# Opening of a two-layer encoder: lighter VectorE work, matrices loaded as rows, power factors on GpSimd

## The chip, the core and the metric

The kernel runs on one core of one Trainium2 chip. The time is the device time of one execution in microseconds (us). The engines are TensorE (PE), VectorE (DVE), ScalarE (ACT), GpSimd (POOL) and the DMA queues, which SyncE (SP), ScalarE and GpSimd feed. All run side by side and wait for each other through semaphores.

## What is computed

A trunk of two pre-norm layers over 256 tokens of width 1024, in float32. Cut to what the change touches:

```python
proj = rms_norm(x, norm_mix[layer]) @ w_in[layer]     # q, k, v, u, gates
q, k = rotary(q), rotary(k)                           # x1*cos - x2*sin, x2*cos + x1*sin per half head
lam = exp(sum(lp[0] * lp[1])) - exp(sum(lp[2] * lp[3])) + lam_init
for direction in range(2):                            # bidirectional diagonal state space mixer
    a_bar = exp(lam_ssm * dt)                         # complex, 32 groups x 64 states
    b_bar = ((a_bar - 1) / lam_ssm)[..., None] * b_mat
    states = linear_scan(a_bar, b_bar @ u)            # 256 steps, reversed in direction 1
    y = y + real(c_mat @ states)
y = y + u * d_skip
```

After each mixer stands a feed-forward part: a SwiGLU in layer 0, top 2 of 8 experts in layer 1.

## The kernel before

Each weight tile (128 x 2048 numbers, 1 MB) is loaded by SyncE, rounded by ScalarE (`hi`, L1215) and its rest taken by VectorE (`lo`, L1632, a split); TensorE then multiplies three times (hi hi, hi lo, lo hi, L657). The order on each engine is written out by hand and the same in both layers: a function `mixer(l)` per engine. A tile's `hi` waits until TensorE has used the tile two before it, and a projection in PSUM (banks PJ) starts when VectorE or ScalarE has signalled `pj_free` for the one before.

The state space mixer works on chunks of four tokens. It needs the input matrices times a_bar to the powers 0 to 4 (`input_power` on VectorE in layer 0, `product` on GpSimd in layer 1), the output matrices likewise (`c_chain`, GpSimd) and tables of phases (`phasors`, `phase_products`, GpSimd; ScalarE mirrors them in `scan_tables`, L1326 and L1332). `inner` (L767, L776, TensorE) forms the products within a chunk; it waits for VectorE's diagonal (`kdiag_ready`), for VectorE's last input power (`b_part`) and for GpSimd's last output power (`c_ready`, the memset of L2232). Then TensorE transposes the input powers (the B turns: eight banks, each evacuated by ScalarE, L1253; ScalarE's mirror copies for the first step stand between the fourth and the fifth). After them comes the loop over eight half heads with scores, softmax, scan steps and the projections of the gates.

In layer 0 the opening runs so. Parameters of the states are worked out as rows and transposed by TensorE into one bank (`par`, L675, seven transposes, before projection t + 2); VectorE copies it (L2002). GpSimd waits for this copy, then does phasors 1 and 2, `c_chain`, phasors 3 and 4, the first phase products. VectorE, after a product and a sum for the attention's lambda (L1998, L1999), works out the four factors co * a^k (`next_factor`, L1734 to L1737, 4 operations each), waits for the raw input matrices, and does power 0; power 1 waits until ScalarE has read the last two banks of the output matrices ("ct", L1308), since it writes where they were loaded. Then come splits, powers 2 to 4, the diagonal and the rotary of q and k in turn. The input matrices are loaded by GpSimd in eight transfers whose runs are 16 numbers, and copied by ScalarE to PSUM banks PY (L1373); the output matrices are loaded twice, in four transfers, so that a 128 x 128 transpose gives both halves. `rotary` multiplies q by cos into SBUF (L1692), the crossed halves by sin into SBUF (L1695, then `pj_free`) and adds the two (L1700).

Of the kernel before, what the change touches and what calls it, by code (L numbers as in the profile page):

```python
# [18 lines left out]
P = 128  # L19
# [23 lines left out]
C_ID, C_TRI, C_ONE, C_IOTA, C_SEL, C_COS, C_SIN = 0, 128, 256, 384, 513, 641, 769  # L43
C_ROW, C_SLOT, C_END = 897, 899, 900
# [79 lines left out]
def build(nc, x, norm_mix, w_in, attn_lambda, attn_subln, ssm_lam_re, ssm_lam_im, ssm_log_dt, ssm_b_re, ssm_b_im,  # L124
# [6 lines left out]
    with ctx:  # L131
# [66 lines left out]
        braw, bbar = powers(area(0, 1024)), powers(area(TMP + 2048, 1024))  # L198
        bt = [powers(area(1024 + 1024 * i, 1024)) for i in range(2)]
        pt = [powers(area(c0, 1024)) for c0 in (14592, TMP)]  # L200
        craw = [area(c0, 1024).rearrange("p (i a s) -> p i a s", i=8, a=2) for c0 in (8192, TMP + 1024)]
# [206 lines left out]
        dve_mark, power_mark = small[:, 20:21], small[:, 21:22]  # L408
        dve_rows, sel_early, inv_ready = sem("dve_rows"), sem("sel_early"), sem("inv_ready")
        B_LOADS, C_LOADS = 16 * 8, 16 * 4  # L410
        den_ready, radius_ready, c_in = sem("den_ready"), sem("radius_ready"), sem("c_in")
# [243 lines left out]
        def _(pe):  # L655
# [137 lines left out]
            def states_numbers_t(l):  # L793

                pe.wait_ge(c_in, C_LOADS * (l + 1))
                for g in range(4):
                    transposes((l, "ct", g), [craw[g // 2][:, 4 * (g % 2) + i, :, :].rearrange("p a s -> p (a s)") for i in range(4)])
# [34 lines left out]
            def mixer(l):  # L832
# [7 lines left out]
                if l == 0:  # L840
                    pe.wait_ge(dve_par, 1)
                    pe.wait_ge(radius_ready, 1)
                    transposes("par", [row(PACK + i) for i in range(7)])
# [364 lines left out]
        def _(act):  # L1208
# [92 lines left out]
            def state_numbers(l):  # L1301

                for g in range(4):
                    bank = wait_turn(act, (l, "ct", g))
                    r, d = g // 2, g % 2
                    for odd in range(2):
                        rows = slice(64 * odd, 64 * (odd + 1))
                        m = act.activation(cblk[rows, r, :, 7 * d, :],  # L1308
                                           bank[rows, :].rearrange("p (j g h) -> p j g h", g=2, h=GC)[:, :, odd, :],
                                           ACT.Copy, scale=1.0 if r == 0 else -1.0)  # L1310
# [30 lines left out]
            def mixer(l):  # L1341
# [28 lines left out]
                if l == 0:  # L1370
                    act.wait_ge(b_in, B_LOADS)
                    for r in range(2):
                        act.activation(PY[r][:, :], braw[:, r].rearrange("p q d h -> p (q d h)"), ACT.Copy).then_inc(braw_full, 1)  # L1373
                    state_numbers(0)
# [251 lines left out]
        def _(dve):  # L1626
# [55 lines left out]
            def rotary(l, name, dst):  # L1682
                i = place_of(l, name)

                cos_t, sin_t = (cst[:, c:c + 128].rearrange("p (t c) -> p t c", t=2) for c in (C_COS, C_SIN))
                for th in range(TH):
                    if th == 0:
                        dve.wait_ge(pj0_full, use(l, i) + 1)
                    else:
                        dve.wait_ge(tile_used, T_MIX[l] + 2 * i + 2)  # L1690
                    src = PJ[th][:, :]
                    own.step(stt(a_flat[:, 0:512].rearrange("p (h c) -> p h c", c=HD), src.rearrange("p (h c) -> p h c", c=HD),  # L1692
                                 col(RI + th), cos_t[:, th, :].unsqueeze(1).broadcast_to([P, 8, HD]), MUL, MUL))
                    for a in range(2):
                        m = stt(a_flat[:, 512:1024].rearrange("p (h a c) -> p h a c", a=2, c=32)[:, :, a, :],  # L1695
                                src.rearrange("p (h a c) -> p h a c", a=2, c=32)[:, :, 1 - a, :], col(RI + th),
                                sin_t[:, th, 32 * a:32 * (a + 1)].unsqueeze(1).broadcast_to([P, 8, 32]), MUL, MUL)
                    m.then_inc(pj_free[th], 1)
                    dve.wait_ge(pj_free[th], pj_read(l, i))
                    tt(dst[:, th, :], a_flat[:, 0:512], a_flat[:, 512:1024], ADD).then_inc(rot_ready, 1)  # L1700
                    dve.wait_ge(rot_ready, 4 * l + (0 if name == "q" else 2) + th + 1)

# [26 lines left out]
            def next_factor(k):  # L1729

                def times(i):
                    return par[:, i:i + 1, 0:32].broadcast_to([P, 2, 32])
                src = par[:, CO_RE:CO_IM + 1, 0:32] if k == 0 else coef[:, k - 1]
                tt(coef_tmp[0], src, times(A_RE), MUL)  # L1734
                own.step(tt(coef_tmp[1], src[:, ::-1, :], times(A_IM), MUL))
# [678 lines left out]
```

## Time and profile before

| | us |
|---|---|
| median of 3 runs (1413.34 to 1413.91) | 1413.44 |
| the profiled execution | 1413.13 |
| its span in the trace | 1411.3 |
| TensorE busy | 1371.2 (97%) |
| VectorE busy | 1107.8 (78%) |
| ScalarE busy | 895.1 (63%) |
| GpSimd busy | 358.3 (25%) |

The shares are means over the whole span, and the stretch that the change touches is its first tenth: between 40 and 80 us VectorE and GpSimd are each busy for more than 19 of every 20 us. What is to be read is which engine ends last there. The chain of waits answers that: it goes back from the last instruction, at each step to what released it. The timeline lists the instructions of an engine in order; a bracket gives the idle time before an instruction and what ended it. An fp32 matmul stands as two records in it, a transpose as one.

### The profile page before, as it was taken

What the parts mean: (1) busy time and instruction counts of PE and PEld (TensorE: products, weight loads), DVE (VectorE), ACT (ScalarE), POOL (GpSimd) and SP (SyncE); (2) the same over time, 40 slices, a digit from 0 to 9 for tenths busy, and PEclk for the clock granted to TensorE, in tenths of its full rate; (3) what the DMA queues carried; (4) which work ended last, traced back from release to release, by engine and by line L of the source; (5) the groups of instructions that cost most, each with busy time, mean ns of one, the idle gap of its engine ahead of it and who ended that gap; (6) DMA issues with size and microseconds to landing.
All of it is one profiled execution on the core that took longest, in us unless ns stands there. A gap on an engine that the chain in (4) does not pass through costs nothing.

```text
span 1411.3 us, 23368 instructions
## 1 busy us (share of the span) xinstructions
PE 1371.2 (97%) x8481; PEld 1122.8 (80%) x8481; DVE 1107.8 (78%) x1021; ACT 895.1 (63%) x903; POOL 358.3 (25%) x459
## 2 busy tenths in 40 slices
PE   6889999999999999999999999999999999999996
PEld 4778778788888787788888888888888888888885
DVE  6987677655556587678888888889888888898886
ACT  5445555444445455556777777777777777777775
POOL 4988718996000187000000000000000000000100
PEclk9999999999999999999999999999999999999998
DMA  9433365655545242697999999999999999999991
GB/s 243 159 95 130 113 187 164 207 181 193 193 168 189 57 172 91 235 330 283 365 373 371 389 377 378 386 359 386 384 365 389 382 373 386 360 383 352 384 355 30
DMA packets 194804, 385.16 MB, mean 273 GB/s; under 512 B 17969, under 2 KB 57265, under 8 KB 194610
## 3 DMA queue, kind: packets, MB, share of 16 engines
q1 hardware_dynamic: 188256, 367.51, 72.9%
q0 software_dynamic: 4336, 14.17, 4.0%
q10 hardware_dynamic: 2146, 2.59, 0.6%
q8 instruction: 43, 0.70, 0.2%
q14 instruction: 23, 0.19, 0.0%
HBM read 375.83 MB, written 7.34 MB: 272 GB/s over the span
## 4 chain that ended last, share of the span: by engine, by line
PE 88%; DVE 5%; ACT 3%; issue 2%; DMA 1%; ACTq 0%; POOL 0%; SPq 0%; DVEq 0%; POOLq 0%
PE bank L657 84%; DVE lo L1632 2%; ACT hi L1215 2%; PE bank L1109 1%; PE bank L675 1%; DMA raw<-in_w_in_dram 1%; PE bank L776 1%; DVE raw L1749 0%; PE bank L1092 0%; DVE bank L1751 0%; PE bank L814 0%; DMA areg<-in_norm_mix_dram 0%; PE bank L983 0%; ACT at_hi L1539 0%; DVE areg L1695 0%
## 5 line engine op out<-in xcount | busy, mean ns | idle before, releaser
L1632 DVE TENSOR_TENSOR lo<-raw,hi 128x2048 fp32r<-128x2048 f32 x347 | 803.1, 2326 | 161.3 <-ACT hi L1215 159.1
L1215 ACT ACTIVATE hi<-raw 128x2048 fp32r<-128x2048 f32 x347 | 663.8, 1916 | 183.9 <-PE bank L657 178.1
L657 PE MATMUL bank<-hi,at_hi 128*128 128x512 f32 x1288 | 513.5, 399 | 13.3 <-DVE lo L1632 8.0
L657 PE MATMUL bank<-hi,at_lo 128*128 128x512 f32 x1288 | 503.4, 391 | 0.0
L657 PE MATMUL bank<-lo,at_hi 128*128 128x512 f32 x1288 | 502.6, 390 | 0.0
L657 PEld LDWEIGHTS bank<-hi,at_hi 128*128 128x128 f32 x1288 | 242.5, 188 | 67.9 <-DVE lo L1632 13.3
L657 PEld LDWEIGHTS bank<-hi,at_lo 128*128 128x128 f32 x1288 | 242.1, 188 | 52.1
L657 PEld LDWEIGHTS bank<-lo,at_hi 128*128 128x128 f32 x1288 | 242.7, 188 | 47.3
L657 PE MATMUL bank<-hi,ht_hi 128*128 128x512 f32 x432 | 168.8, 391 | 0.9 <-DVE ht_lo L2116 0.9
L657 PE MATMUL bank<-hi,ht_lo 128*128 128x512 f32 x432 | 168.1, 389 | 0.0
L657 PE MATMUL bank<-lo,ht_hi 128*128 128x512 f32 x432 | 168.1, 389 | 0.0
L2343 POOL TENSOR_TENSOR small<-cst 128x1 f32<-128x1 f32 x14 | 5.9, 422 | 590.7 <-DVE slot_row L2153 298.6
L657 PEld LDWEIGHTS bank<-hi,ht_hi 128*128 128x128 f32 x432 | 81.1, 188 | 19.2 <-DVE lo L1632 1.5
L657 PEld LDWEIGHTS bank<-hi,ht_lo 128*128 128x128 f32 x432 | 81.1, 188 | 17.0
L657 PEld LDWEIGHTS bank<-lo,ht_hi 128*128 128x128 f32 x432 | 81.1, 188 | 16.6
L1548 ACT ACTIVATE ht_hi<-bank 128x512 fp32r<-128x512 f32 (+1 forms) x48 | 26.9, 560 | 55.6 <-PE bank L1109 55.6
L2273 POOL TENSOR_TENSOR raw<-raw 128x256 f32<-128x256 f32 x64 | 46.8, 762 | 21.6 <-ACT raw L1332 7.6
L1544 ACT ACTIVATE vreg<-bank 128x512 f32<-128x512 f32 (+1 forms) x48 | 27.1, 565 | 25.1 <-PE bank L657 25.1
L657 PEld LDWEIGHTS bank<-raw 64*64 64x64 f32 x1152 | 36.1, 134 | 7.6 <-issue 4.4
L657 PE MATMUL bank<-raw 64*64 64x64 f32 x1152 | 40.5, 221 | 0.0
L2266 POOL MEMSET raw<- 128x4 f32 x4 | 0.3, 104 | 151.9 <-DVE raw L1726 151.9
L1227 ACT ACTIVATE at_hi<-bank 128x512 fp32r<-128x512 f32 x32 | 17.7, 596 | 33.3 <-PE bank L675 33.3
(304 smaller groups left out, 1150.8 us busy)
## 6 DMA issues: line engine op xcount, KB each, us to landing
raw<-in_moe_w_dram SPq DMA_DIRECT2D x528, 512.0 KB, 6.8
raw<-in_ffn_w_dram SPq DMA_DIRECT2D x66, 512.0 KB, 4.2
raw<-in_w_in_dram SPq DMA_DIRECT2D x64, 512.0 KB, 4.5
raw<-in_w_branch_dram SPq DMA_DIRECT2D x16, 512.0 KB, 4.4
raw<-in_w_out_dram SPq DMA_DIRECT2D x16, 512.0 KB, 4.7
raw<-in_w_glu_dram SPq DMA_DIRECT2D x4, 512.0 KB, 4.1
moe_sum<-xres POOLq DMA_DIRECT2D x3, 512.0 KB, 5.4
xres<-in_x_dram SPq DMA_DIRECT2D x2, 512.0 KB, 6.5
```

The source lines that it names most:

```text
L657: return pe.matmul(o, a, b, start=start, stop=stop)
L675: last = pe.transpose(bank[:, i * rows:(i + 1) * rows], src, ident[0:rows, 0:rows])
L776: m = pe.matmul(bank[r0:r0 + GC, c0:c0 + 64], bbar[rows, r, q, d, :], cblk[rows, r, q, 4 * d:4 * d + 4, :].rearrange("p i h -> p (i h)"), ...
L1109: m = pe.transpose(TR[0][:, f * P:(f + 1) * P], v_flat[:, f * P:(f + 1) * P], ident)
L1215: act.activation(hi[:, slot, :], src, ACT.Copy).then_inc(hi_ready, 1)
L1227: act.activation(at_hi[:, k0:k0 + kn, c0:c0 + P], bank[:, 0:kn * P].rearrange("p (k c) -> p k c", k=kn), ACT.Copy, scale=scale).then_inc(a ...
L1544: act.activation(v_flat[:, 0:h_width(c)], PJ[0][:, 0:h_width(c)], ACT.Silu).then_inc(g_ready, 1)
L1548: act.activation(ht_rows_hi[:, 0:h_width(c) // P, :], TR[0][:, 0:h_width(c)].rearrange("p (f s) -> p f s", s=P), ACT.Copy).then_inc(ht_hi_ ...
L1632: tt(lo[:, slot, :], src, hi[:, slot, :].bitcast(f32), SUB).then_inc(lo_ready, 1)
L2266: pool.memset(edge[:, :, :, 0:1], 0.0)
L2273: last = tt(dst, src[:, :, :, d, :], w[:, r:r + 1, :, d, :].broadcast_to([P, 2, 2, 64]), MUL)
L2343: tt(small[:, 82 + i:83 + i], ident[:, 0:1], ident[:, 0:1], MUL).then_inc(pool_passed, 1)
```

## The change

Eight edits, one of them in both layers' mixers (rotary), one at the end of layer 0 too (the output matrices):

- The input matrices of layer 0 are loaded as rows, in two transfers (`brow`, 64 partitions each, rows of 1024 numbers), and TensorE brings them into PY itself with 64 products by columns of the identity (`raw_matrices`), before it transposes the parameters. The two ScalarE copies go.
- The output matrices are loaded once per part, and each half is its own product by a part of the identity (64 stationary columns, 64 moving), so that ScalarE evacuates a bank with one operation over 128 partitions instead of two over 64.
- ScalarE copies `par` instead of VectorE.
- `next_factor` runs on GpSimd, ahead of its phasors; VectorE waits for `coef_ready` before powers 1 to 4.
- The sum for lambda runs on GpSimd, ahead of `par`, as a product and six halving additions; VectorE's use of it moves behind the first row maximum.
- The diagonal is one operation over 128 partitions with a table of units; GpSimd clears `dskip` first.
- `rotary` does the crossed halves first, then multiplies by cos in place in PSUM, then adds the PSUM bank and the crossed halves; `pj_free` is signalled behind the addition by a memset.
- The table of cosines is half as wide.

```diff
-C_ID, C_TRI, C_ONE, C_IOTA, C_SEL, C_COS, C_SIN = 0, 128, 256, 384, 513, 641, 769
-C_ROW, C_SLOT, C_END = 897, 899, 900
+C_ID, C_TRI, C_ONE, C_IOTA, C_SEL, C_COS, C_SIN = 0, 128, 256, 384, 513, 641, 705
+C_ROW, C_SLOT, C_UNIT, C_END = 833, 835, 836, 852
...
+brow = area(0, 1024).rearrange("p (s h) -> p s h", h=GC)
...
-craw = [area(c0, 1024).rearrange("p (i a s) -> p i a s", i=8, a=2) for c0 in (8192, TMP + 1024)]
+craw = [area(c0, 512).rearrange("p (i s) -> p i s", i=8) for c0 in (8192, TMP + 1024)]
...
-B_LOADS, C_LOADS = 16 * 8, 16 * 4
-den_ready, radius_ready, c_in = sem("den_ready"), sem("radius_ready"), sem("c_in")
+B_LOADS, C_LOADS = (16 * 2, 16 * 10), 16 * 2
+den_ready, radius_ready, c_in, coef_ready = sem("den_ready"), sem("radius_ready"), sem("c_in"), sem("coef_ready")
...
         pe.wait_ge(c_in, C_LOADS * (l + 1))
         for g in range(4):
-            transposes((l, "ct", g), [craw[g // 2][:, 4 * (g % 2) + i, :, :].rearrange("p a s -> p (a s)") for i in range(4)])
+            bank = open_turn((l, "ct", g))
+            for i in range(4):
+                for odd in range(2):
+                    m = mm(bank[64 * odd:64 * odd + 64, 64 * i:64 * i + 64], craw[g // 2][:, 4 * (g % 2) + i, :],
+                           ident.rearrange("p (j g h) -> p j g h", g=2, h=GC)[:, :, odd, :], True, True)
+            m.then_inc(tr_full, 1)
+    def raw_matrices():
+        pe.wait_ge(b_in, B_LOADS[0])
+        for r in range(2):
+            rows = slice(64 * r, 64 * r + 64)
+            for h in range(GC):
+                for g in range(2):
+                    o = PY[r][64 * g:64 * g + 64, :].rearrange("p (q d h) -> p d q h", q=PAIRS, d=2)[:, :, :, h]
+                    m = mm(o, brow[rows, :, h], ident[rows, 64 * r + g:64 * r + 64:2], True, True)
+            m.then_inc(braw_full, 1)
...
         proj(t + 1, l, 0, 4, False, True)
         if l == 0:
+            raw_matrices()
             pe.wait_ge(dve_par, 1)
             pe.wait_ge(radius_ready, 1)
             transposes("par", [row(PACK + i) for i in range(7)])
...
-            for odd in range(2):
-                rows = slice(64 * odd, 64 * (odd + 1))
-                m = act.activation(cblk[rows, r, :, 7 * d, :],
-                                   bank[rows, :].rearrange("p (j g h) -> p j g h", g=2, h=GC)[:, :, odd, :],
-                                   ACT.Copy, scale=1.0 if r == 0 else -1.0)
+            m = act.activation(cblk[:, r, :, 7 * d, :], bank[:, 0:256].rearrange("p (q h) -> p q h", h=GC),
+                               ACT.Copy, scale=1.0 if r == 0 else -1.0)
...
-            act.wait_ge(b_in, B_LOADS)
-            for r in range(2):
-                act.activation(PY[r][:, :], braw[:, r].rearrange("p q d h -> p (q d h)"), ACT.Copy).then_inc(braw_full, 1)
+            bank = wait_turn(act, "par")
+            act.activation(par[:, :, :].rearrange("p i (l q d) -> p (i l) q d", l=2, q=PAIRS),
+                           bank[:, 0:448].rearrange("p (x d q) -> p x q d", d=2, q=PAIRS),
+                           ACT.Copy).then_inc(tr_free[TURN["par"] % 2], 1)
             state_numbers(0)
...
-        cos_t, sin_t = (cst[:, c:c + 128].rearrange("p (t c) -> p t c", t=2) for c in (C_COS, C_SIN))
+        cos_t = cst[:, C_COS:C_COS + HD].rearrange("p (t c) -> p t c", t=2)
+        sin_t = cst[:, C_SIN:C_SIN + P].rearrange("p (t c) -> p t c", t=2)
         for th in range(TH):
             if th == 0:
                 dve.wait_ge(pj0_full, use(l, i) + 1)
             else:
                 dve.wait_ge(tile_used, T_MIX[l] + 2 * i + 2)
             src = PJ[th][:, :]
-            own.step(stt(a_flat[:, 0:512].rearrange("p (h c) -> p h c", c=HD), src.rearrange("p (h c) -> p h c", c=HD),
-                         col(RI + th), cos_t[:, th, :].unsqueeze(1).broadcast_to([P, 8, HD]), MUL, MUL))
+            crossed = a_flat[:, 512 * th:512 * th + 512]
             for a in range(2):
-                m = stt(a_flat[:, 512:1024].rearrange("p (h a c) -> p h a c", a=2, c=32)[:, :, a, :],
+                m = stt(crossed.rearrange("p (h a c) -> p h a c", a=2, c=32)[:, :, a, :],
                         src.rearrange("p (h a c) -> p h a c", a=2, c=32)[:, :, 1 - a, :], col(RI + th),
                         sin_t[:, th, 32 * a:32 * (a + 1)].unsqueeze(1).broadcast_to([P, 8, 32]), MUL, MUL)
-            m.then_inc(pj_free[th], 1)
-            dve.wait_ge(pj_free[th], pj_read(l, i))
-            tt(dst[:, th, :], a_flat[:, 0:512], a_flat[:, 512:1024], ADD).then_inc(rot_ready, 1)
+            own.step(m)
+            halves = src.rearrange("p (h c) -> p h c", c=32)
+            own.step(stt(halves, halves, col(RI + th), cos_t[:, th, :].unsqueeze(1).broadcast_to([P, 16, 32]), MUL, MUL))
+            tt(dst[:, th, :], src, crossed, ADD).then_inc(rot_ready, 1)
             dve.wait_ge(rot_ready, 4 * l + (0 if name == "q" else 2) + th + 1)
+            dve.memset(bank_mark, 0.0).then_inc(pj_free[th], 1)
...
-    def next_factor(k):
...
         t1 = bt[0]
+        if k > 0:
+            dve.wait_ge(coef_ready, k)
...
-        for g in range(2):
-            rows = slice(64 * g, 64 * g + GC)
-            last = tt(kdiag[rows], cst[rows, C_ID + 64 * g:C_ID + 64 * g + GC].unsqueeze(1).broadcast_to([GC, PAIRS, GC]),
-                      dskip[rows, l, :].unsqueeze(2).broadcast_to([GC, PAIRS, GC]), MUL)
-        last.then_inc(kdiag_ready, 1)
+        tt(kdiag, cst[:, C_UNIT:C_UNIT + GC].unsqueeze(1).broadcast_to([P, PAIRS, GC]),
+           dskip[:, l, :].unsqueeze(2).broadcast_to([P, PAIRS, GC]), MUL).then_inc(kdiag_ready, 1)
...
             wait_read(dve, "par")
-            for k in range(4):
-                next_factor(k)
             dve.wait_ge(braw_full, 2)
             input_power(whole(bbar), 0)
...
+            dve.wait_ge(lam_ready, 1)
             input_power(b_power(1), 1)
...
-        if l == 0:
-            dve.wait_ge(lam_exp, 1)
-            le = col(LEXP, 4).rearrange("p (l a) -> p l a", l=2)
-            own.step(tt(col(NLAM, 2), le[:, :, 1], le[:, :, 0], SUB))
-            for i in range(2):
-                lam_init = 0.8 - 0.6 * math.exp(-0.3 * i)
-                own.step(ts(col(NLAM + i), col(NLAM + i), -lam_init, None, ADD))
-                own.step(ts(subln[:, i, :], subln[:, i, :], 1.0 - lam_init, None, MUL))
         for s in range(8):
             row_max(l, s)
+            if l == 0 and s == 0:
+                dve.wait_ge(lam_exp, 1)
+                le = col(LEXP, 4).rearrange("p (l a) -> p l a", l=2)
+                own.step(tt(col(NLAM, 2), le[:, :, 1], le[:, :, 0], SUB))
+                for i in range(2):
+                    lam_init = 0.8 - 0.6 * math.exp(-0.3 * i)
+                    own.step(ts(col(NLAM + i), col(NLAM + i), -lam_init, None, ADD))
+                    own.step(ts(subln[:, i, :], subln[:, i, :], 1.0 - lam_init, None, MUL))
...
-    dve.wait_ge(lam_in, 32)
-    own.step(tt(lamp.rearrange("p (l a) c -> p l a c", l=2), lamv[:, :, :, 0, :], lamv[:, :, :, 1, :], MUL))
-    dve.tensor_reduce(col(LSUM, 4), lamp, AX.X, ADD).then_inc(lam_ready, 1)
     dve.wait_ge(loads, 16)
-    bank = wait_turn(dve, "par")
-    dve.tensor_copy(par[:, :, :].rearrange("p i (l q d) -> p (i l) q d", l=2, q=PAIRS),
-                    bank[:, 0:448].rearrange("p (x d q) -> p x q d", d=2, q=PAIRS)).then_inc(tr_free[TURN["par"] % 2], 1)
...
-            for a in range(2):
-                pool.dma_start(craw[r][:, :, a, :], src[l, :, :, :, :].rearrange("d g h s -> (d g h) s")
-                               .rearrange("(i p) s -> p i s", p=P)).then_inc(c_in, 16)
+            pool.dma_start(craw[r], src[l, :, :, :, :].rearrange("d g h s -> (d g h) s")
+                           .rearrange("(i p) s -> p i s", p=P)).then_inc(c_in, 16)
...
+    def next_factor(k):
+        def times(i):
+            return par[:, i:i + 1, 0:32].broadcast_to([P, 2, 32])
+        src = par[:, CO_RE:CO_IM + 1, 0:32] if k == 0 else coef[:, k - 1]
+        tt(coef_tmp[0], src, times(A_RE), MUL)
+        own.step(tt(coef_tmp[1], src[:, ::-1, :], times(A_IM), MUL))
+        tt(coef[:, k, 0], coef_tmp[0][:, 0], coef_tmp[1][:, 0], SUB)
+        tt(coef[:, k, 1], coef_tmp[0][:, 1], coef_tmp[1][:, 1], ADD).then_inc(coef_ready, 1)
+        pool.wait_ge(coef_ready, k + 1)
     pool.memset(gain[0:32, :], 0.0).then_inc(row_zero, 1)
     pool.wait_ge(rows_in, 48)
     tt(row(R_t), row(R_LR), row(R_LR), MUL)
     own.step(tt(row(R_u), row(R_LI), row(R_LI), MUL))
     tt(row(R_den), row(R_t), row(R_u), ADD).then_inc(den_ready, 1)
     pool.wait_ge(raw_full[1], 32)
-    load_matrices(0)
+    for r, src in enumerate((ssm_b_re, ssm_b_im)):
+        pool.dma_start(brow[64 * r:64 * r + 64, :, :],
+                       src[0, :, :, :, :].rearrange("d g s h -> (d g) s h")).then_inc(b_in, 16)
     load_states(0)
     pool.wait_ge(act_par, 2)
     radius = row(PACK + RAD4)
     own.step(tt(radius, row(R_er), row(R_er), MUL))
     tt(radius, radius, radius, MUL).then_inc(radius_ready, 1)
+    own.step(pool.memset(dskip[:, :, :], 0.0))
     load_dskip(0)
     load_dskip(1)
+    pool.wait_ge(lam_in, 32)
+    own.step(tt(lamp.rearrange("p (l a) c -> p l a c", l=2), lamv[:, :, :, 0, :], lamv[:, :, :, 1, :], MUL))
+    for w in (32, 16, 8, 4, 2):
+        own.step(tt(lamp[:, :, 0:w], lamp[:, :, 0:w], lamp[:, :, w:2 * w], ADD))
+    tt(col(LSUM, 4), lamp[:, :, 0], lamp[:, :, 1], ADD).then_inc(lam_ready, 1)
     wait_read(pool, "par")
+    for k in range(4):
+        next_factor(k)
...
-            pool.wait_ge(b_in, B_LOADS * 2)
+            pool.wait_ge(b_in, B_LOADS[1])
...
+    for g in range(2):
+        c[64 * g:64 * g + GC, C_UNIT:C_UNIT + GC] = np.eye(GC)
...
-    c[:, C_COS:C_COS + P] = np.concatenate([np.cos(ang), np.cos(ang)], -1).reshape(P, P)
+    c[:, C_COS:C_COS + HD] = np.cos(ang).reshape(P, HD)
```

## Rows read from the trace of the kernel before

**Rows 1.** Page, chain that ended last: shares of the span by engine.
```profile
PE 88%; DVE 5%; ACT 3%; issue 2%; DMA 1%; ACTq 0%; POOL 0%; SPq 0%; DVEq 0%; POOLq 0%
```

**Rows 2.** Chain in order of time, opening: start us, duration us, engine, tile, line.
```profile
34.83 0.34 DVE gates L1998
...
39.93 1.29 DVE raw L1749 x2
...
43.77 1.29 DVE raw L1749 x2
...
78.99 0.33 PE bank L767 x8
...
96.28 11.68 PE bank L657 x136
107.96 0.37 PE bank L814 x2
```

**Rows 3.** Timeline of VectorE: start, duration us, line, operation, shapes, count.
```profile
60.48 0.75 DVE L1692 SCALAR_TENSOR_TENSOR areg<-bank,small,cst 128x512 f32<-128x512 f32 x1
...
62.17 1.05 DVE L1700 TENSOR_TENSOR qk<-areg 128x512 f32<-128x512 f32 x1
...
77.11 1.62 DVE L1765 TENSOR_TENSOR raw<-cst,small 16x256 f32<-16x256 f32 x2
...
105.50 0.48 DVE L1784 SCALAR_TENSOR_TENSOR qk<-bank,small,qk 128x256 f32<-128x256 f32 x1
```

**Rows 4.** Timeline of GpSimd, opening; idle time before and its releaser in brackets.
```profile
36.23 0.34 POOL L464 TENSOR_TENSOR raw<-par 128x64 f32<-128x64 f32 x1 [7.80 <-DVE par L2002]
...
37.44 0.29 POOL L475 COPY raw<-php_last 128x64 f32<-128x64 f32 x1
...
48.53 3.24 POOL L448 TENSOR_TENSOR raw<-raw 128x512 f32<-128x512 f32 x1
51.73 1.29 POOL L449 TENSOR_TENSOR raw<-raw 128x512 f32<-128x512 f32 x1
...
62.63 1.75 POOL L449 TENSOR_TENSOR raw<-raw 128x512 f32<-128x512 f32 x1
...
73.77 0.10 POOL L2232 MEMSET small<- 128x1 f32 x1
...
89.70 0.45 POOL L2255 TENSOR_TENSOR raw<-php_last 128x128 f32<-128x128 f32 x1
```

**Rows 5.** Timeline of ScalarE: C copies and the first mirror copies.
```profile
39.41 3.14 ACT L1308 ACTIVATE raw<-bank 64x256 f32<-64x256 f32 x8 [4.74 <-PE bank L675]
...
91.65 0.50 ACT L1332 ACTIVATE raw<-raw 128x128 f32<-128x128 f32 x2
```

**Rows 6.** Timeline of TensorE, opening.
```profile
31.01 0.65 PE L675 MATMUL bank<-cst,gates 64*128 64x64 f32 x7
33.22 0.47 PE L657 MATMUL bank<-hi,at_hi 128*128 128x512 f32 x1 [1.55 <-ACT ureg L1266]
...
38.77 1.04 PE L675 MATMUL bank<-cst,raw 128*128 128x128 f32 x8
...
47.08 1.99 PE L657 MATMUL bank<-cst,ureg 64*32 64x64 f32 x128
...
74.81 1.03 PE L675 MATMUL bank<-cst,qk 128*128 128x128 f32 x8
...
86.87 2.08 PE L657 MATMUL bank<-cst,raw 64*64 64x64 f32 x64 [0.34 <-ACT qk L1472]
```

**Rows 7.** One microsecond of `inner`: busy us of each engine, granted clock, DMA.
```profile
80.00:81.00 1.00, 1.00 (x48) 1.00 (x44) 0.97 (x3) 0.00 (x0) 1.00 (x2) 0.50 0.00 0
```

**Rows 8.** Chain in order of time, layer 1, q's rotary.
```profile
460.39 0.89 DVE areg L1695 x2
...
461.42 11.17 PE bank L657 x48
```

**Rows 9.** Waits of TensorE's weight loads: for whom, total us, times, longest.
```profile
PEld bank L675 <- ACT raw L1308: 2.1, 4, 0.7
```

More of the change, by code:

```diff
@@ L407, in build @@
         xn_hi, xn_lo = (a[:, (T_MOE + 2) % SPLITS, :].rearrange("p (t d) -> p t d", t=TH) for a in (hi, lo))
-        dve_mark, power_mark = small[:, 20:21], small[:, 21:22]
+        dve_mark, power_mark, bank_mark = small[:, 20:21], small[:, 21:22], small[:, 18:19]
         dve_rows, sel_early, inv_ready = sem("dve_rows"), sem("sel_early"), sem("inv_ready")
-        B_LOADS, C_LOADS = 16 * 8, 16 * 4
-        den_ready, radius_ready, c_in = sem("den_ready"), sem("radius_ready"), sem("c_in")
+        B_LOADS, C_LOADS = (16 * 2, 16 * 10), 16 * 2
+        den_ready, radius_ready, c_in, coef_ready = sem("den_ready"), sem("radius_ready"), sem("c_in"), sem("coef_ready")
         KC_LOADS = 16 * 16
@@ L1727, in scanned @@
                 last.then_inc(zs_ready, 1)
-            def next_factor(k):
[L1731 to L1735, printed above, removed]
-                tt(coef[:, k, 0], coef_tmp[0][:, 0], coef_tmp[1][:, 0], SUB)
-                own.step(tt(coef[:, k, 1], coef_tmp[0][:, 1], coef_tmp[1][:, 1], ADD))
             def input_power(dst, k):
```

## Prediction

> **What bounds the kernel now.** I read the page's chain that ended last first: TensorE (PE) holds 88% of it and VectorE (DVE) 5% [rows 1]. So only what moves TensorE's start of some stretch counts. The chain by time shows where VectorE enters: from 34.83 to 78.99 us every link but one projection is VectorE (lambda product, copy of the parameters, four factors, five input powers, four splits, q's rotary, diagonal); TensorE then starts `inner` at 78.99 and the loop over the heads at 96.28 [rows 2]. From there the chain is TensorE without a pause through layer 0's loop. The opening therefore has one result that matters, the 96.28 us; behind it I look for single places where TensorE waits for something edited.
>
> The next view is the timeline of each engine in the opening, to see who is second. GpSimd starts at 36.23, when the parameters arrive, and then has no pause: the c powers end at 73.77 (`mark(c_ready)`, for which `inner` waits too) and the first phase products (`wtab_half`) at 89.70 + 0.45 = 90.15 [rows 4]. ScalarE (ACT) mirrors them at 91.65 [rows 5], between the evacuations of B banks 1 and 2, so it has 1.5 us to spare. That is all the slack GpSimd has. This is the point of the argument: VectorE is first by little, and the change gives GpSimd work ahead of exactly this chain.
>
> **VectorE, what goes.** The lambda product and sum, the copy of `par` and the 16 small operations of `next_factor` fill 34.83 to 39.93 us [rows 2], the factors some 3.7 of them: 5.1 us ahead of the first input power. The diagonal becomes one 128x256 operation; the nearest row is the lambda product, 128x256 too, 0.34 us of the chain [rows 2], so I take 0.45 with its wait for 1.63 (77.11 to 78.74 [rows 3]): 1.2 us less. q's rotary: per half 0.75 (main part), 0.89 (crossed parts) and 1.05 (sum of two SBUF operands) [rows 3, 8], with gaps 2.8. New: 0.89, then 0.75 in place in PSUM (the same operation but for where it writes; between 0.7 and 0.8), some 0.7 for the sum, which now reads PSUM as the main part does, and some 0.16 for two added waits and the mark: 2.5. Two halves save 0.6.
>
> **TensorE, what comes ahead of `par`.** `raw_matrices` is 64 fp32 products with a 64x64 stationary and 32 moving columns, queued before the transposes of the parameters, which start at 31.01 now [rows 6]. An fp32 product stands as two records (the u transposes are 64 products and 128 records), so 128 records. The rows give per record: u transposes, 64x32 stationary, 1.99/128 = 15.5 ns; B transposes, 64x64 stationary, 2.08/64 = 32, start to start 30; full 128x128 transposes 1.04/8 = 130 ns, of which half the columns would be 65 [rows 6]. Ends: 2.0 us and 8.3 us. I take the B transposes, the same stationary size: 29 ns x 128 = 3.7 us. Its data are no limit: the b loads are two transfers of 4 KB rows in place of eight of 64 byte runs, issued by 17 us, needed at 31. So `par`'s transposes run 34.8 to 35.45, ScalarE copies them by 36.1 (its copies of this size take about what VectorE's did), and the parameters arrive at 36.1: the same time as now. What VectorE no longer does ahead of them, TensorE does. A weight tile that lands earlier through the lighter transfers would move VectorE's fourth split, which ends before 34.83 [rows 2] in any case; I count that at nothing, since the raw products cover it. If they took 2.0 us, it would be worth nothing either, for the copy would come at 34.4.
>
> In sentences that the sum does not need: the Trainium skill (Advanced Engine Details and Errata, "Memory Cachelines") says that any non-contiguous access pattern in PSUM slows matmuls and that SBUF reads which touch a new 16 byte line each time pay. `raw_matrices` does both: its stationary has a step of 16 floats and its output one of 16 and 32. No matmul of the trace before is of this form; the rule speaks against 3.7 us and is rival 1.
>
> **VectorE after `par`.** Power 0 runs 36.15 to 40.0 (3.84 us, 39.93 to 43.77 [rows 2]). Power 1 waits for C banks 2 and 3. The projection that started at 33.22 [rows 6] now starts at 35.5, so the C products begin at 38.77 + 2.3 = 41.1. Four banks at 16 records x 29 ns = 0.46 each (as now: 8 transposes in 1.04), four ScalarE copies of 128x256 instead of eight of 64x256 (3.14/8 = 0.39 each [rows 5]), interleaved: read by 43.35. So power 1 starts at 43.4 instead of 43.77: of the 5.1 us removed, 3.4 turn into this wait and 1.3 into the later start. From there to the diagonal's end there are 34.97 us now, less 0.6 and 1.2: VectorE is done at 76.6 instead of 78.74.
>
> **GpSimd.** Lambda (seven small operations) and the memset lie in its idle 7.80 us before 36.23 [rows 4], hidden. `next_factor` x4 lies behind `par` and in front of the phasors. A complex product of this size takes 1.21 us there (four operations from 36.23 to the copy at 37.44 [rows 4]), so +4.85 us; from below VectorE's own 3.7 bounds it, from above 6.0 with a quarter more for waits. Given back: GpSimd stalls while VectorE reads two SBUF operands. 3.24 us at 48.53 against 1.29 at 51.73 beside a split; 1.75 at 62.63 beside the rotary sum [rows 4]. Four such rotary sums and the diagonal go; 0.45 each, 1.75 until 90.15, 0.9 of them until 73.77. So `c_ready` is at 73.77 + 4.85 - 0.9 = 77.7 and `wtab_half` at 90.15 + 4.85 - 1.75 = 93.25.
>
> **TensorE after that.** `inner` starts at 77.75, held by GpSimd and no longer by VectorE: -1.25. It ran its first half at a granted clock of 0.5 [rows 7], the lower level, 1.2 GHz, after an idle stretch from 75.84 to 78.99 [rows 6]; the idle stretch is now 74.7 to 77.75, so I leave its price as it is. The B turns reach ScalarE's mirror copies at 90.5, where it must wait until 93.3 instead of going on at 91.65. From the mirror to the loop are 96.28 - 91.65 = 4.63; one bank's fill (32 records, 0.95) is gained, as two banks fill meanwhile. Loop: 93.3 + 4.63 - 0.95 = 97.0, against 96.28: **+0.7 us**. The lambda work now stands behind the first row maximum and makes the first head's weights up to 1.8 us later on VectorE; they end at 105.98 [rows 3] and TensorE transposes them at 107.96 [rows 2], from now on 0.7 later: 0.9 us remain, no cost. If more than that were lost, each microsecond would count in full.
>
> **Elsewhere.** End of layer 0, C products of layer 1: TensorE's loads wait for ScalarE's copies, 2.1 us in four waits, two per layer [rows 9]: 1.05. With half the copies the wait is about 0.4: **-0.6** (ends: -1.0, and +0.9 if a record with 128 rows costs 55 ns). Layer 1, q's rotary: TensorE starts its projection at 461.42 right behind VectorE's crossed parts (460.39 + 0.89 [rows 8]), having waited for `pj_free`. That signal now comes after the in-place product, the sum and the mark: 459.61 + 2.5 = 462.1, start 462.25: **+0.85** (ends 0.7 and 1.0), with nothing behind it to hide it since the chain stays on TensorE. k's rotary in layer 1 and both in layer 0 have no projection waiting within a microsecond. Behind layer 1 nothing changes but shapes of constants.
>
> **Sum.** +0.7 - 0.6 + 0.85 = +0.95. Against the profiled run, 1413.13 us (span 1411.3), that is 1414.1; the three runs' median is 0.3 above the profiled one. I forecast 1414.3.
>
> **Rivals.**
> 1. Strided products are slow (the other side): 58 to 65 ns per record, `raw_matrices` 7.4 to 8.3 us instead of 3.7. Everything behind `par` (GpSimd, power 1, `inner`) moves by as much: +3.7 to +4.6, C products in layer 1 too: 1418 to 1419. For it: the form is new here. Against: the array is fed at half rate in fp32 anyhow. It decides from about 5.5 us on. By this figure the time would leave the 0.2% band.
> 2. The products overlap as the u transposes do, 2.0 us. The parameters come at 34.4, everything is 1.7 earlier: loop at 95.3, sum -0.75, 1412.6. TensorE then stands idle for 3 us at the B turns, about as long as the stretch before `inner` after which the clock fell, which would cost back up to 1.3 us: 1412.6 to 1413.9.
> 3. GpSimd isn't the bound (its factors take less, or the relief is larger) and `inner` starts early enough to keep 2.4 GHz. Then -1.25 - 1.35 (half of the 2.7 us that the first bank's 128 records take at the 48 in a microsecond of [rows 7]) and the B turns unhindered: -2.6 to -4.3, 1409 to 1411. Against: GpSimd has no pause from 36 to 90.
>
> VectorE does get lighter in each of these, by 7 us; what they differ in is whether any of it reaches TensorE.
>
> **How the numbers follow.** Forecast 0.48, alone 1412.8 to 1415.8; rival 1 0.24; rival 2 0.16; rival 3 0.12. Two in ten left out: 1411.0 to 1418.2. What a measurement of this kernel can tell from no change is 0.2%, 2.8 us. Rival 3 gives faster in most of its cases, 0.12; rival 1 gives slower in most of its cases, 0.22; same 0.66.
>
> **What would show it.** In the trace after: the factors on GpSimd about 36.2 to 41 us; VectorE idle ahead of the second input power by some 3 us, for ScalarE's C copies; TensorE released into `inner` by GpSimd's mark; ScalarE waiting about 2.8 us for GpSimd before the first mirror; the loop's first score at 97; in layer 1 the projection behind q's rotary waiting 1.4 us instead of 0.6. It would be wrong if `raw_matrices` took far from 3.7 us, if GpSimd's first mark came before 76, or if TensorE waited inside the loop.

## The result and the profile after

Median 1418.39 us (1417.36 to 1421.16, 9 runs) against 1413.83 us (1412.34 to 1416.11, 9 runs): ratio 1.0037, 95% interval 1.0029 to 1.0046. The change makes the kernel 0.37% slower: 5.2 us by the ratio, 4.6 between the two medians. The profiled run took 1417.42 us (span 1415.6, before 1411.3).

The chain of the kernel after, 28 to 102 us (start us, us, engine and line), is to be compared with [rows 2]. In the kernel before, VectorE filled the opening. In the kernel after, the chain runs over TensorE and ScalarE's copy of the parameters, and from there over GpSimd almost up to the loop's start:

```profile
27.93 9.45 PE bank L658 x130
37.38 0.95 PE bank L676 x7
38.36 0.55 ACT par L1387
38.98 0.32 POOL raw L2285
...
43.84 0.31 POOL raw L465
...
95.26 0.42 POOL raw L2253
95.70 0.51 ACT raw L1347 x2
96.21 0.49 ACT raw L1271
96.75 2.08 PE bank L658 x64
98.83 0.74 issue
99.57 2.38 PE bank L658 x36
```

TensorE's timeline of the kernel after (start us, us, line, operation, shapes, count) is to be compared with [rows 6]: the 128 records of `raw_matrices` take 6.96 us from 30.35 to the transposes of the parameters, 54 ns each where the forecast had 29; those transposes stood at 31.01 before. The C products start at 46.52 instead of 38.77.

```profile
30.35 7.03 PE L658 MATMUL bank<-cst,raw 64*64 64x32 f32 x128
37.31 1.01 PE L676 MATMUL bank<-cst,gates 64*128 64x64 f32 x7
46.52 2.32 PE L658 MATMUL bank<-cst,raw 128*64 128x64 f32 x64
...
82.25 0.30 PE L768 MATMUL bank<-raw,cst 16*16 16x64 f32 x8 [1.62 <-DVE raw L1773]
82.48 1.98 PE L777 MATMUL bank<-raw 64*16 64x64 f32 x128
...
86.67 1.51 PE L777 MATMUL bank<-raw 64*16 64x64 f32 x91 [1.32 <-issue]
```

Windows of the same stretch (window, its length, TensorE busy and its records in brackets, granted clock as a share of 2.4 GHz, DMA share, GB/s): the clock falls to 1.2 GHz during the products, in which TensorE is never idle, and stays there through most of the projection behind them:

```profile
30.00:33.00 3.00, 3.00 (x50) 1.00 0.22 55
33.00:34.00 1.00, 1.00 (x30) 0.78 0.81 219
34.00:36.00 2.00, 2.00 (x44) 0.50 1.00 379
...
42.00:44.00 2.00, 2.00 (x7) 0.55 0.00 0
44.00:46.00 2.00, 2.00 (x11) 1.00 0.01 4
```

VectorE and ScalarE of the kernel after [rows 3, 5]. VectorE waits 6.66 us for the C copies ahead of its second input power, which starts at 49.46 instead of 43.77; ScalarE waits 1.27 us for GpSimd ahead of its first mirror copies, at 95.70 instead of 91.65:

```profile
38.99 1.29 DVE L1759 TENSOR_TENSOR raw<-bank,par 128x512 f32<-128x512 f32 x2 [4.74 <-ACT par L1387]
49.46 1.29 DVE L1759 TENSOR_TENSOR raw<-bank,raw 128x512 f32<-128x512 f32 x2 [6.66 <-ACT raw L1324]
...
95.70 0.51 ACT L1347 ACTIVATE raw<-raw 128x128 f32<-128x128 f32 x2 [1.27 <-POOL raw L2253]
```

The waits of TensorE from 455 to 475 us (total, times, longest); at this place, behind q's rotary in layer 1, it waited 0.6 us in the kernel before [rows 8]:

```profile
PE bank L658 <- DVE small L1719: 1.5, 1, 1.5
```

Inside the loop of layer 0 TensorE waits once for GpSimd, in the second head, which it did not before:

```profile
117.80 1.38 PE L658 MATMUL bank<-raw 64*64 64x64 f32 x40 [0.26 <-POOL raw L2278]
```

So the span's +4.3 us are: loop of layer 0 at 99.57 instead of 96.28, +3.3; +0.3 inside that loop by its third head, with that wait; +0.3 more up to the C products of layer 1 (225.45 instead of 221.53), which was not followed up; those products -0.4 (2.26 us up to the next projection, 2.66 before); q's rotary in layer 1 +0.9.

### The profile page after: what moved, and what is told of

Read it like the earlier page. It is cut to its first block, busy times and chain, and to the rows that moved or that the text cites. A ratio compares the mean times of both kernels' runs of the same rounds, so it can differ in the third digit from the quotient of the medians.

```text
span 1415.6 us, 23801 instructions
## 1 busy us (share of the span) xinstructions
PE 1379.9 (97%) x8705; PEld 1130.6 (80%) x8705; DVE 1099.2 (78%) x1008; ACT 891.3 (63%) x894; POOL 357.6 (25%) x473
## 4 chain that ended last, share of the span: by engine, by line
PE 87%; POOL 5%; DVE 3%; ACT 2%; issue 2%; DMA 0%; ACTq 0%; POOLq 0%
PE bank L658 83%; DVE lo L1648 2%; PE bank L1127 1%; ACT hi L1233 1%; PE bank L676 1%; POOL raw L444 1%; POOL raw L446 1%; POOL raw L2271 1%; POOL raw L465 0%; PE bank L1110 0%; POOL raw L466 0%; PE bank L1001 0%; ACT at_hi L1555 0%; DMA areg<-in_norm_mix_dram 0%; PE bank L831 0%
```

## Experiments

Each ran in turns with the kernel before; a ratio is to that kernel. "Parameters" is GpSimd's first operation behind their copy, "inner" TensorE's first product of `inner`, "mirror" ScalarE's first mirror copy, "loop" the first score of layer 0; all four times are us of the one profiled execution, the ratio is from all of them. Such a time scatters: up to the parameters nothing differs between after, e3, e6 and e12, and they came at 38.98 to 40.39; between before and e9 neither, and they came at 36.23 and 34.73. The profiled execution can also lie above the median of its kernel, by 2.1 us in e1 and in e9.

| kernel | ratio (95%) | parameters | inner | mirror | loop |
|---|---|---|---|---|---|
| before | 1 | 36.23 | 78.99 | 91.65 | 96.28 |
| after | 1.0037 (1.0029 to 1.0046) | 38.98 | 82.25 | 95.70 | 99.57 |
| e1_old_b | 1.0010 (1.0002 to 1.0019) | 34.48 | 76.73 | 91.49 | 96.91 |
| e2_par_first | 1.0026 (1.0014 to 1.0038) | 33.38 | 81.51 | 93.39 | 98.01 |
| e3_factors_dve | 1.0026 (1.0015 to 1.0036) | 40.39 | 82.48 | 94.36 | 98.99 |
| e6_rot_old | 1.0076 (1.0063 to 1.0089) | 39.80 | 82.60 | 98.14 | 102.79 |
| e9_before_factors | 1.0028 (1.0016 to 1.0039) | 34.73 | 77.45 | 93.01 | 97.74 |
| e10_par_ct_first | 0.9988 (0.9979 to 0.9997) | 34.20 | 75.49 | 87.60 | 92.39 |
| e11_contig_timed | 1.0017 (1.0008 to 1.0026) | 36.47 | 78.48 | 93.26 | 97.13 |
| e12_rot_layer1_old | 1.0034 (1.0021 to 1.0046) | 39.67 | 81.68 | 96.45 | 100.32 |
| e13_ct_behind | 0.9979 (0.9970 to 0.9988) | 34.79 | 75.85 | 87.83 | 92.64 |
| e14_rot_all_old | 0.9988 (0.9979 to 0.9997) | 35.07 | 77.00 | 89.17 | 93.96 |

**Without the strided products (e1_old_b).**

```
-                    raw_matrices()
+            load_matrices(0)            # eight loads, on GpSimd's queue
+                    for r in range(2):  # on ScalarE, behind the copy of the parameters
+                        act.activation(PY[r][:, :], braw[:, r]..., ACT.Copy).then_inc(braw_full, 1)
```

> The changed kernel with the input matrices of layer 0 loaded and copied as before (eight loads, two ScalarE copies), without the 64 strided products. Theory (the products cost 7.0 us and the slow clock behind them; GpSimd and VectorE both pass it on): the parameters arrive at about 34 us instead of 38.9, GpSimd's first phase products end at about 90.8 instead of 95.7, the second input power starts at about 44 instead of 49.5 and inner at about 76.6 instead of 82.3; the loop starts at about 94.5 instead of 99.6, and the time is about 1413.4. Rival (the loss comes from the factors on GpSimd, the products being hidden): loop at 99 or later, 1417.5 to 1418.5.

Measured 1414.96 us against 1413.22. The parameters, the second input power (43.73) and `inner` came as the theory said, and most of the loss went. The loop did not: TensorE waited 2.18 us for GpSimd, through ScalarE, and the granted clock then fell, so that 64 B products took 3.63 us instead of 2.08 (TensorE's timeline; the windows 92 to 94 and 94 to 96 show 0.64 and 0.50):

```profile
92.54 3.63 PE L658 MATMUL bank<-cst,gates 64*64 64x64 f32 x64 [2.18 <-ACT raw L1270]
```

The theory had left this out: GpSimd as the bound costs its own lateness and, at times, the clock. Only this execution has a trace, and e1's eleven took 1412.44 to 1418.10 us; how many of them lost the clock is not shown.

**The parameters first (e2_par_first), the factors back on VectorE (e3_factors_dve).**

```
+                    transposes("par", [row(PACK + i) for i in range(7)])
                     raw_matrices()
-                    transposes("par", [row(PACK + i) for i in range(7)])
```

> The changed kernel with the strided products behind the transposes of the parameters instead of ahead of them; same work. Theory (two paths are late, and VectorE's, through the projection and the C copies, is not helped by this): parameters at about 34 us, GpSimd's first phase products at about 90.8, so ScalarE's wait of 1.27 us before the first mirror goes; the second input power and inner start as late as now (49.5, 82.3); loop at about 98.4, 1417.3. Rival (the late parameters alone make the loss): loop 4.9 us earlier, 1413.5.

```
-            for k in range(4):
-                next_factor(k)          # GpSimd
+                    for k in range(4):
+                        next_factor(k)  # VectorE, ahead of input_power(whole(bbar), 0)
```

> The changed kernel with the four factors back on VectorE, ahead of the first input power. Theory (two late paths): VectorE takes them, 3.7 us, out of its 6.7 us of waiting for the C copies, so the second input power starts at 49.5 as now; GpSimd is 4.85 us earlier; inner at 82.3 as now, loop at about 98.4, 1417.3. Rival (the factors on GpSimd are the loss): loop at about 95, 1413.5.

Measured 1416.85 and 1417.05 us against 1413.22: both as the theory had it, neither rival. Early parameters, or a GpSimd rid of 4.85 us, are worth 1.3 to 1.5 us by the medians, with intervals that overlap that of the change, because VectorE is late as well, over another path: products, slowed projection, C products, C copies, second power (48.95 us in e2, 49.91 in e3, 49.46 in the kernel after). In e3 the factors fit into VectorE's wait, which leaves `inner` where it was.

**Which stride costs (e7_forms_a and e8_forms_b, one execution each; e11_contig_timed).** The stationary is the operand that a weight load brings into TensorE, the moving operand the one that streams against it.

```
-                            m = mm(o, brow[rows, :, h], ident[...:2], True, True)
+ e7, r == 0: stationary area(0, 1024)[rows, 64 * h:64 * h + 64]; result as now
+ e7, r == 1: stationary brow[rows, :, h]; result PY[r][64 * g:64 * g + 64, 32 * h:32 * h + 32]
+ e8, e11   : stationary and result both in a row
```

> The changed kernel with two other forms of the 64 products, so the input matrices of layer 0 come out in another order: the first 64 records read a contiguous stationary (64 floats in a row) and write as now (step 16 and 32 floats), the last 64 read the stationary as now (step 16 floats) and write 32 columns in a row. Now: 54.9 ns per record for both halves together. Theory (the stationary's step costs, loads of 181 to 223 ns against 135): about 30 ns for the first half, 50 to 55 for the second. Rival (the step in the result costs): the other way round.

> The changed kernel with the products' stationary and result both contiguous; the first half still reads its moving operand with a step of 2 floats, the second half reads 32 columns in a row (the input matrices of layer 0 are not what they should be). Theory: 29 ns per record or less in both halves, as the forecast took it from the B transposes, 3.7 us in all, and the granted clock stays at its upper level in them; the parameters arrive at about 35.6 us. Rival (small products cost this much in any form at this place, or the moving operand's step costs): 50 ns or more in the first half at least.

> The same kernel as e8_forms_b (products with contiguous stationary and result; the input matrices of layer 0 are not what they should be), timed. Theory (only the size of one term was off, 7.0 us for 3.7): loop at 96.8 us, 1414.3 within 1.5, that is 0.1% above the kernel before. Rival (some of the loss has another cause): 1416.5 or more.

TensorE's weight loads in e7 (group, count, busy us, mean ns), L814 with the contiguous stationary and strided result, L818 the reverse; then its matmuls around the turn from the one form to the other:

```profile
L818 PEld LDWEIGHTS bank<-cst,raw 64*64 64x64 f32 x64 | 3.7, 202 | 0.0
L814 PEld LDWEIGHTS bank<-cst,raw 64*64 64x64 f32 x64 | 1.9, 135 | 0.4 <-issue 0.4
```

```profile
31.23 1.88 PE L814 MATMUL bank<-cst,raw 64*64 64x32 f32 x58
32.90 0.30 PE L818 MATMUL bank<-cst,raw 64*64 64x32 f32 x2
...
33.15 3.56 PE L818 MATMUL bank<-cst,raw 64*64 64x32 f32 x60
36.64 1.01 PE L676 MATMUL bank<-cst,gates 64*128 64x64 f32 x7
```

Start to start: (32.90 - 31.23)/58 = 28.8 ns per record with the strided result, (36.64 - 33.15)/60 = 58 ns with the strided stationary. The latter is the load's price, 202 against 135 ns for one, and about the same at either clock (in the kernel after a load takes 203 ns between 30.3 and 33.5 us, at 2.4 GHz, and 204 between 34.0 and 37.2, at 1.2). The step in the result costs nothing, and neither does the moving operand's step of 2 floats, which e8's first half still has: (32.68 - 31.01)/58 = 28.8 ns. In e8 all 128 records take 34.66 - 31.01 = 3.65 us:

```profile
31.01 1.88 PE L814 MATMUL bank<-cst,raw 64*64 64x32 f32 x58
32.68 0.25 PE L817 MATMUL bank<-cst,raw 64*64 64x32 f32 x2
...
34.66 0.80 PE L676 MATMUL bank<-cst,gates 64*128 64x64 f32 x7
...
78.14 0.30 PE L768 MATMUL bank<-raw,cst 16*16 16x64 f32 x8 [1.55 <-DVE raw L1778]
...
96.78 0.67 PE L658 MATMUL bank<-qk,ureg 64*128 64x256 f32 x2 [0.74 <-issue]
```

With the term at the size forecast, `inner` and the loop stand at 78.14 and 96.78 where the prediction had 77.75 and 97.0. e7 took 1416.76 us and e8 1414.68 in their one run; timed as e11, e8 took 1414.86 us against 1413.28 (forecast: 1414.3). The part of the expectation that failed is the clock: it fell right behind these products too, from 35 to 38.5 us.

**The factors alone, on the kernel before (e9_before_factors).** The diff's move of `next_factor`, nothing else.

> The kernel before with one edit: the four factors go to GpSimd ahead of its phasors. Theory (GpSimd's chain had 1.5 us to spare): its first phase products end at about 95 instead of 90.2, the loop starts at 98.7 instead of 96.3, and where TensorE waits over 2 us at the B turns the granted clock falls and up to 3.5 us more are lost: 1415.5 to 1419. Rival (VectorE sets the loop, GpSimd follows it): VectorE's 3.7 us come free, no loss: 1411 to 1413.5.

Measured 1416.83 us against 1412.40, ratio 1.0028: the move by itself makes that kernel slower. VectorE is 1.5 us earlier at `inner`, which is no more than the 1.5 us by which the parameters came earlier in this execution; its 3.7 us went into a wait of 3.04 us for the C copies and a diagonal that took 1.2 us longer. ScalarE then waits 3.29 us for GpSimd, TensorE 2.40 for ScalarE. The clock falls behind that wait: 64 B products take 2.95 us, and the loop's first 136 records, 11.68 us in [rows 2], 15.08 (chain of e9, start, us):

```profile
93.01 0.51 ACT raw L1332 x2
93.52 0.49 ACT raw L1253
94.06 2.95 PE bank L657 x64
97.00 0.74 issue
97.74 15.08 PE bank L657 x136
```

**The rotary (e6_rot_old, e12_rot_layer1_old).** The old order in both layers, or in layer 1 alone; the half table of cosines stays:

```
+                        own.step(stt(a_flat[:, 0:512]..., halves, col(RI + th), cos_t...))
+                        ... crossed parts to a_flat[:, 512:1024]
+                        m.then_inc(pj_free[th], 1)
+                        tt(dst[:, th, :], a_flat[:, 0:512], a_flat[:, 512:1024], ADD)
```

> The changed kernel with both rotaries in the old order (main part and crossed parts to SBUF, then the bank is given free, then the sum of two SBUF operands). Theory: in layer 1 the projection behind q's rotary starts 0.85 us earlier relative to the loop of layer 0; in the opening VectorE is 0.6 us later and some of it reaches inner; in all 0.3 to 0.85 less, 1417.5 to 1418.1. Rival (the free signal is hidden by other work): no gain in layer 1, 1418.4 to 1419.

> The changed kernel with the rotaries of layer 1 in the old order and those of layer 0 in the new one. Theory: the opening is as in the changed kernel, loop at 99.6; TensorE's wait for the bank behind q's rotary in layer 1 goes from 1.5 back to 0.6 us; 0.85 less than the changed kernel, 0.28 to 0.35% above the kernel before, 1417 to 1417.8. What the earlier run with all rotaries old lost then belongs to the opening. Rival (the loss of that run lies in the new view of the cosines or in layer 1): 2 us or more above the changed kernel.

e12 took 1417.03 us, as expected, and TensorE's wait in layer 1 is back at 0.6:

```profile
PE bank L658 <- DVE areg L1725: 0.6, 1, 0.6
```

e6 was a miss by 6 us: 1424.18 us. Its layer 1 is as e12's (the same wait of 0.6 us), so the loss lies in the opening. GpSimd's chain from the end of the factors to the mirror took 98.14 - 44.68 = 53.5 us, against 95.70 - 43.84 = 51.9 in the kernel after; TensorE waited 2.54 us and the clock fell, as the lengths show (e6's timeline, then the chain of its loop):

```profile
99.18 2.86 PE L658 MATMUL bank<-cst,gates 64*64 64x64 f32 x64 [2.54 <-ACT raw L1271]
```

```profile
102.79 15.18 PE bank L658 x136
```

Of the 3.2 us by which its loop starts later, 1.6 are GpSimd's slower chain, 0.8 later parameters (scatter, since nothing ahead of them is edited) and 0.8 the B products at 1.2 GHz; another 3.5 are the clock inside the loop. The new order in layer 0 thus gives GpSimd 1.6 us, where the prediction counted 0.6 for VectorE.

**A version that beats both (e10_par_ct_first, e13_ct_behind, e14_rot_all_old).** The changed kernel with the input matrices as in e1, the factors as in e3, the rotary of layer 1 as in e12; in e10 the C products also stand ahead of the projection, in e14 the rotary of layer 0 is the old one as well.

```
                 if l == 0:
+                    states_numbers_t(0)              # e10 only
                 proj(t + 2, l, 1, 0, True, False)
-                if l == 0:
-                    states_numbers_t(0)              # e10 only
...
+                    if l == 0 ...new order...        # e10, e13
+                    else ...old order...             # e14: old order for both
```

> A version made from the findings: the change's lighter parts kept (C loaded once, one copy for each C bank, parameters copied by ScalarE, lambda on GpSimd, diagonal in one, rotary in layer 0 in the new order), the input matrices loaded as before, the factors on VectorE, the C products ahead of the projection instead of behind it, and the rotary of layer 1 in the old order. Theory: parameters at 33.5, GpSimd's first phase products at 87, VectorE's diagonal done at 75.6, inner at 75.9 right behind the transposes of q at the upper clock, loop at 92.6 to 93.7, 0.4 us less at layer 1: 1409 to 1410.5. Rival (what VectorE gains is lost to GpSimd's slower operations beside it): loop not before 95.5, 1412 to 1413.5.

> The version of e10_par_ct_first with the C products behind the projection again, as in the changed kernel. Theory: VectorE's factors (3.7 us) lie in its wait for the C copies, so the second input power starts at 43.6 either way and the loop at 93 to 94, against 92.4: within 1 us of it, 1410.5 to 1412. Rival (having the C products first is what brings the gain): loop at 96, 1413.5 or more.

> The version of e13_ct_behind with the old rotary order in layer 0 as well. The same edit on the changed kernel (e6_rot_old) cost 5.5 us or so, 1.6 of them because GpSimd's chain took longer beside VectorE and the rest by the granted clock behind the wait that came of it. Theory: here GpSimd's chain has about 4 us to spare, so its longer time is hidden; only VectorE's 0.6 us reaches inner: loop at 93.2, the same time as e13_ct_behind within 1 us, 0.1 to 0.2% below the kernel before. Rival (the old order costs by itself, wherever GpSimd stands): 4 us or more above e13_ct_behind, 1414 to 1416.

Measured 1410.99 us against 1412.40, 1410.19 against 1413.28, 1411.01 against 1413.15. e13 is 0.21% below the kernel before (0.12 to 0.30%). e10 came 0.5 us above its expected range and e13 0.3 below. The place of the C products makes no difference that the two intervals show. In e13 GpSimd is no longer on the path: its mark comes at 71.84 us with `inner` at 75.85, and ScalarE's mirror copies wait for nothing:

```profile
71.84 0.10 POOL L2254 MEMSET small<- 128x1 f32 x1
```

```profile
75.85 0.30 PE L768 MATMUL bank<-raw,cst 16*16 16x64 f32 x8 [1.75 <-DVE raw L1795]
76.08 1.98 PE L777 MATMUL bank<-raw 64*16 64x64 f32 x128
...
92.64 0.67 PE L658 MATMUL bank<-qk,ureg 64*128 64x256 f32 x2 [0.74 <-ACT raw L1270]
```

In e14 the old rotary costs about 1 us (0.9988 against 0.9979) where in e6 against e12 it cost 6 (1.0076 against 1.0034): where GpSimd has slack, its slower operations are hidden, and with them the fall of the clock. e10's profiled span is 4.0 us below the kernel before, its median only 1.4; what its other runs lost is open.

## Why the prediction was wrong

The predicted 1414.3 us was 4.1 low, and the result lies 0.2 us above the range. It was rival 1 (1418 to 1419, chance 0.24) that came about. In part its number is luck: it had 7.4 us or more for the products, which took 7.0, and nothing for the clock; 3.3 us more on the forecast would be 1417.6.

- **The step that failed: "I take the B transposes, the same stationary size: 29 ns x 128 = 3.7 us".** It measured 7.0. The row was chosen by the size of the stationary, but the stationary of that row loads in 135 ns, as the contiguous one of e7 does; what sets the price here is the step of 16 floats in the loads. e8 and e11 show that this term separates the forecast from the result: with it at 3.65, `inner` and the loop come within 0.4 us of the forecast in e8, within 0.8 in e11, and the time with them.
- **The rule behind rival 1 is half borne out.** The Trainium skill (Advanced Engine Details and Errata, "Memory Cachelines") says that reads of SBUF which touch a new 16 byte line each time pay: the stationary does so, and doubles the price, 28.8 to 58 ns; that 16 bytes is the edge no run here shows. It also says that any non-contiguous pattern in PSUM slows matmuls significantly: in e7 a result with steps of 16 and 32 floats ran at 28.8 ns per record, the pace of the contiguous one in e8. For this form the measurement decides against it.
- **What followed the 3.3 us.** The forecast's projection at full clock ran at 1.2 GHz, 8.3 us from 38.25 to the C products against 5.6 before: 2.7 more. So the C products began 5.4 us behind the 41.1 forecast, and the second power 6.1. The parameters were 2.8 late. The two paths, over VectorE and over GpSimd, were late by nearly the same; e2 and e3 each mend one and gain 1.3 to 1.5 us. Taking the products away does not always bring the clock back: in e1 it fell from 34.5 to 38 us behind an idle 2.39 us, while in e13 and e14 it kept 2.4 GHz behind 1.91 and 1.88 us.
- **GpSimd: right.** Factors 43.84 - 38.98 = 4.86 us (4.85). Relief: from the phasors to the mirror or the end of the products 53.9 us before, 51.9 after, 2.0 (1.75). That GpSimd's chain sets the loop once it has the factors is shown by e9: from the parameters to the loop it takes 63.0 us where the kernel before takes 60.1, close to the 4.85 us of the factors less the 1.5 of slack, while VectorE reaches `inner` no later.
- **`inner`: wrong on who releases it and on the clock.** GpSimd's mark came at 80.28 us and VectorE's diagonal released TensorE at 82.25, behind the late second power; the forecast had GpSimd ahead there. ScalarE's wait for GpSimd ahead of the mirror is 1.27 us and not 2.8 for that reason. The first 128 records ran at 2.4 GHz, 1.98 us for 3.52 (rival 3 put that gain at 1.35), and most of the gain went into a gap of 1.32 us in the second bank, 0.32 before. The gap is 0.8 to 1.0 us in e8, e11 and e13; what fills it was not tried.
- **From mirror to loop: right.** 99.57 - 95.70 = 3.87 (3.68). **The lambda work behind the first row maximum: put at nothing, and not quite nothing.** The first head's weights are transposed 3.3 us later, as late as the loop. But the chain goes back from TensorE's wait of 0.26 us in the second head over GpSimd and ScalarE to VectorE, whose five lambda operations stand between the row maximum and the split and take 2.0 us there. Where they take 1.5 to 1.8 us (e1, e10, e13, e14), TensorE does not wait. The prediction had named a wait inside the loop as a sign of being wrong.
- **C products of layer 1: right in sign,** -0.4 (-0.6). **q's rotary in layer 1: right,** 1.5 - 0.6 = +0.9 (+0.85), and e12 takes it back.
- **The clock behind a late GpSimd: missing in the forecast.** Rival 2 alone priced it, at up to 1.3 us at the B turns. In the kernel after it did not matter (a wait of 0.38 us, clock at 2.4 GHz); the profiled execution of e9 shows 0.9 + 3.4 = 4.3.

## What to carry to other kernels

When a new small matmul is priced from a row of the trace, match the steps of its operands, the stationary's above all, not only its shape: here the stride doubled a term that stood ahead of everything. Before work is given to an engine that "is not the bound", count its slack at the point where the bound waits for it; here it was 1.5 us for 4.85 us of work, and the same lighter code with the factors left on VectorE, the input matrices loaded as they were and layer 1's rotary in the old order (e13) is 0.2% faster than the kernel before. Where two paths are late together, undoing either shows little, so undo both before calling one innocent.

## What the runs showed of the hardware

- The granted clock fell without any idle time of TensorE: during the 128 strided products (from 33.7 us, kernel after), and 0.3 us behind the contiguous ones (from 35, e8). Without such products the transposes and the projection behind them kept 2.4 GHz in e9, e14 and e13, across waits of 1.16, 1.88 and 1.91 us, and did not in e1, across 2.39.
- At the B turns the clock fell behind waits of 2.18 (e1), 2.40 (e9) and 2.54 us (e6), and not behind 1.95 (e12), 2.04 (e8) or 2.23 (e11). A wait near this length cost nothing, 1.6 us (e1) or 4.3 us (e9, e6). That is why an edit worth 1.6 us to GpSimd, the rotary's order in layer 0, moved the time by 6.
- Strided loads take as long at 2.4 as at 1.2 GHz (203 and 204 ns, kernel after): they hid the low clock while they ran, and the projection behind them paid for it.
